# Two-network inference kernel on one core: steps of the recurrent layer's end, the final branch and the expert gather in another order and form

## The chip, the cores and the metric

The kernel runs on one core of one Trainium2 chip. The time is the device time of one execution in microseconds (us), of which the median of several runs is given. TensorE (PE) multiplies, VectorE (DVE) and ScalarE (ACT) work on what it leaves in its eight PSUM banks, GpSimd (POOL) works on SBUF alone, and SyncE (SP) issues the loads of the weights.

## The reference, cut to what matters

Two small transformer stacks stand one behind the other, on 256 tokens of width 1024. The first has two layers (a GQA mixer and an MLA mixer, each with a convolutional feed-forward part). The second has two layers: layer 0 mixes with a chunked gating unit beside a recurrent layer (RWKV-7) and ends in a SwiGLU; layer 1 mixes with sparse attention beside a short convolution and ends in a mixture of 8 experts, of which each token takes 2. The change touches the end of the recurrent layer, the experts, and the final norm.

```python
# layer 0 of the second stack
ya = _chunked_sgu(...)                    # 512 columns
yb = _rwkv7_time_mix(...)                 # 512 columns: recurrence, then a norm per head, bonus and gate
h = h + concatenate([ya, yb]) @ e_w_out[i]
...
def _moe_swiglu(h, w_router, b_router, w_gate, w_up, w_down):
    logits = xf @ w_router + b_router
    top_val, top_idx = lax.top_k(logits, TOP_K)          # TOP_K = 2 of N_EXPERTS = 8
    gates = jax.nn.softmax(top_val, axis=-1)
    ...                                                  # rows of each expert gathered
    return (jax.nn.silu(xb @ w_gate[e]) * (xb @ w_up[e])) @ w_down[e]   # EXPERT_DIM = 1408
...
return _rms_norm(h, final_norm)
```

## The kernel before

**Layout.** Activations lie transposed: `x` and `h` hold 8 tiles of 128 features by 512 columns, of which the second stack uses the 256 columns of the real tokens. Each engine has a program of its own that is written out by hand (`tensor`, `scalar`, `vector`, `gpsimd`, `sync`), and semaphores named by events (`did`, `at`) tie them together. Nothing is scheduled by a planner: what stands first in an engine's program is done first.

**Weights.** All weights come in the order of use as 1 MB chunks through a ring of 4 (`load_chunks` on SP). A chunk is two units of 128x1024. Nearly all products are made to about fp32 precision from two fp32r parts (fp32r is the type of the one-pass product; plain f32 operands take two matmul records each in the profile): `hi_units` on ACT writes the high part of a unit (`WHI`), `lo_units` on DVE subtracts it from the unit to get the low part (`WLO`), and `mm3` on PE adds three products (high by high, high by low, low by high) at L77, L78 and L79. There are 4 buffers for units, so ACT can be at most 4 units ahead, and a ring slot is free again when its second low part is made.

**End of the recurrent layer.** `solve_*` runs the recurrence for two chunks of 128 tokens (c = 0, 1). The norm of chunk 0 is done in between (the `early` generators). What is left behind the solve is `rwkv_out_*`: on PE `mean_pe(1)`, `var_pe(1)` and `roots_pe(1)`, each waiting for DVE or ACT (centre, square, root, reciprocal), then `scale_out_dve(1)`, `gate_out_dve(1)` and the two parts of the result in `HHI` and `HLO`. Only then comes `out_pe` for `e_w_out`: `project_block` makes 4 groups of output columns at once, over k = 0 to 7, with 12 matmuls for each k. Of these, k = 0 to 3 need only the gating unit's half (`yl` 0 to 3, low parts made by POOL), k = 4 to 7 need both chunks of the recurrent half (`yl` 4 and 5). The first four units of `e_w_out` are prepared by ACT and DVE behind the solve.

**Experts.** `router_*` computes logits, the two experts of each token and the places of the tokens, and `HT`, the tokens turned to rows in plain f32. `experts` then runs over e = 0 to 7 in the order `up(i)`, perhaps `scatter`, `gather(i + 1)`, `down(i - 1)`. `gather(e)` on PE multiplies `HT` with the 0/1 matrix `PP` of expert e (16 f32 matmuls of 128 columns); ACT takes the high part from PSUM (`XSHI`), DVE the low part (`XSLO`). Behind them PE turns `PP` (`PPT`, for the scatter) and makes the gate of each gathered token (`GP`). `up(e)` is three blocks of 512, 512 and 384 columns for gate and up weights each, `down(e)` two groups of 512 columns, over 33 units per expert together. The second operand of `XSP` has room for two experts, so gathering for e + 1 and using e do not collide.

**End.** The last squares and sums give the final norm's root (ACT) and reciprocal (DVE, `recip_dve(11)`). If an expert had over 128 tokens, a second pass over all experts follows (`second_pass`, an If on each engine with an Else that raises the skipped semaphores); it is not run here. PE then spreads the reciprocal (`spread_pe(12)`), DVE applies it to 8 tiles, and SP and ACT store one half each.

```python
def second_pass(lane, most, done, body):
    lane.wait_ge(*at(*done))           # PE: ss 11 7, ACT: root 11, DVE: rt 11
    with lane.e.If(most > CAP):
        body(lane, 1)
```

## Time and profile before

| what | us |
|---|---|
| median of 3 runs (2142.18 to 2147.69) | 2145.52 |
| the profiled execution | 2143.13 |
| its span | 2141.2 |
| around the span (2143.13 - 2141.2) | 1.9 |

The profile is one execution. The rows of a timeline give start, length, engine, line and operation of instructions in order of time, and in brackets how long the engine had been idle and what released it. PE rows give the matmuls; as they are pipelined, the pace is read from the distance of two starts and not from a row's length. Lines are those of helpers, so instructions are told by their tiles: `R` and `SM` are working areas, `C` and `CR` constants, `ps` a PSUM bank. A matmul of plain f32 operands shows as two records.

### The profile page before, as it was taken

Reading aid. Unit: us, or ns where it says so; the run is one execution under the profiler, and the core shown is the slowest. Engines: PE = TensorE matmul, PEld = TensorE weight load, DVE = VectorE, ACT = ScalarE, POOL = GpSimd, SP = SyncE. Lnnn points to the kernel's source line nnn. Section 1 sums busy time; section 2 is a strip of 40 time slices with the busy share of each in tenths; the row PEclk is TensorE's granted clock in tenths of the full one; section 3 lists DMA queues with packets and bytes.
Section 4 is the critical chain, followed back from the end, with each engine's and each line's share of the span. In section 5 each row is a group of like instructions: output and inputs, shape, how many; then the busy total and the mean of one; then the engine's idle time right before and its main releaser. Section 6 shows DMA issues by size and latency. Waiting matters only on the chain.

```text
span 2141.2 us, 32979 instructions
## 1 busy us (share of the span) xinstructions
PE 1999.1 (93%) x13572; PEld 1705.9 (80%) x13572; DVE 1318.8 (62%) x1992; ACT 1050.2 (49%) x1688; POOL 293.4 (14%) x303
## 2 busy tenths in 40 slices
PE   5999889999999899999998979999888899999997
PEld 2775568888778756899988869999876788888886
DVE  3238545776454458577557545444566678888886
ACT  3246533333344236566446324444445567676774
POOL 1201132111000410322013212111101000000000
PEclk9999999999999899999999889999998999999998
DMA  8332443554222121255534013545442578888783
GB/s 330 115 122 99 158 177 118 196 179 175 86 91 99 46 98 41 99 180 191 199 139 157 3 41 129 185 173 198 167 184 71 193 293 323 324 314 334 311 327 149
DMA packets 52669, 364.83 MB, mean 170 GB/s; under 512 B 5920, under 2 KB 8224, under 8 KB 8864
## 3 DMA queue, kind: packets, MB, share of 16 engines
q1 hardware_dynamic: 49488, 357.06, 45.2%
q10 hardware_dynamic: 3024, 5.58, 0.7%
q8 instruction: 110, 1.80, 0.3%
q14 instruction: 47, 0.39, 0.1%
HBM read 361.57 MB, written 1.05 MB: 169 GB/s over the span
## 4 chain that ended last, share of the span: by engine, by line
PE 83%; DVE 8%; issue 3%; ACT 3%; POOL 2%; DMA 1%; DVEq 0%; POOLq 0%; ACTq 0%; SPq 0%
PE ps L77 22%; PE ps L79 21%; PE ps L78 21%; PE ps L74 17%; DVE WLO L91 3%; PE ps L82 2%; ACT R L85 1%; DVE SM L105 1%; DVE R L91 1%; POOL R L91 1%; POOL h L95 1%; ACT WHI L85 1%; DMA ring<-W 1%; DVE x L88 0%; DVE h L88 0%
## 5 line engine op out<-in xcount | busy, mean ns | idle before, releaser
L91 DVE TENSOR_TENSOR WLO<-ring,WHI 128x1024 fp32r<-128x1024 f32 x557 | 674.7, 1247 | 203.3 <-ACT WHI L85 202.6
L85 ACT ACTIVATE WHI<-ring 128x1024 fp32r<-128x1024 f32 x557 | 567.9, 1053 | 114.7 <-PE ps L79 112.8
L77 PE MATMUL ps<-HHI,WHI 128*128 128x256 f32 (+1 forms) x1680 | 545.3, 325 | 29.8 <-DVE HLO L88 15.0
L78 PE MATMUL ps<-HLO,WHI 128*128 128x256 f32 (+1 forms) x1744 | 557.0, 319 | 0.0
L79 PE MATMUL ps<-HHI,WLO 128*128 128x256 f32 (+1 forms) x1680 | 538.3, 320 | 0.0
L77 PEld LDWEIGHTS ps<-HHI,WHI 128*128 128x128 f32 x1680 | 326.9, 195 | 69.5 <-issue 38.7
L78 PEld LDWEIGHTS ps<-HLO,WHI 128*128 128x128 f32 x1744 | 339.4, 195 | 20.0
L79 PEld LDWEIGHTS ps<-HHI,WLO 128*128 128x128 f32 x1680 | 326.3, 194 | 21.4
L74 PE MATMUL ps<-R 64*64 64x64 f32 (+9 forms) x2736 | 224.0, 286 | 5.6 <-ACT R L85 2.5
L74 PEld LDWEIGHTS ps<-R 64*64 64x64 f32 (+4 forms) x2736 | 167.6, 155 | 45.3 <-issue 36.3
L85 ACT ACTIVATE R<-ps 128x256 f32<-128x256 f32 (+5 forms) x240 | 113.0, 474 | 158.3 <-PE ps L74 94.5
L85 ACT ACTIVATE R<-ps,VEC 128x512 f32<-128x512 f32 (+1 forms) x106 | 69.1, 660 | 244.3 <-PE ps L79 243.1
L91 POOL TENSOR_TENSOR R<-R 128x256 f32<-128x256 f32 (+1 forms) x99 | 106.5, 1078 | 556.4 <-ACT R L85 555.9
L88 DVE SCALAR_TENSOR_TENSOR R<-ps,VEC,R 128x510 f32<-128x510 f32 (+1 forms) x176 | 107.9, 616 | 99.6 <-ACT R L85 95.6
L77 PE MATMUL ps<-WHI,XSHI 128*128 128x512 f32 (+3 forms) x416 | 154.9, 372 | 4.5 <-DVE WLO L91 4.2
L79 PE MATMUL ps<-WHI,XSLO 128*128 128x512 f32 (+3 forms) x416 | 150.4, 362 | 0.0
L78 PE MATMUL ps<-WLO,XSHI 128*128 128x512 f32 (+3 forms) x416 | 150.1, 361 | 0.0
L91 POOL TENSOR_TENSOR HLO<-h,HHI 128x256 fp32r<-128x256 f32 (+1 forms) x69 | 68.6, 1004 | 330.8 <-ACT HHI L85 328.4
L82 PEld LDWEIGHTS ps<-C,R 128*128 128x128 f32 x504 | 59.5, 145 | 56.2 <-issue 24.5
L77 PE MATMUL ps<-HID,WHI 128*128 128x256 f32 x352 | 100.2, 285 | 0.0
L82 PE MATMUL ps<-C,R 128*128 128x128 f32 x504 | 74.1, 286 | 27.4 <-DVE R L95 8.2
L79 PE MATMUL ps<-HID,WLO 128*128 128x256 f32 x352 | 99.6, 283 | 0.0
(171 smaller groups left out, 2819.0 us busy)
## 6 DMA issues: line engine op xcount, KB each, us to landing
ring<-W SPq DMA_DIRECT2D x340, 1024.0 KB, 4.9
x<-xt ACTq DMA_DIRECT2D x1, 2048.0 KB, 14.8
CR<-const_nsa ACTq DMA_DIRECT2D x1, 560.0 KB, 5.7
out<-x SPq DMA_DIRECT2D x1, 512.0 KB, 3.0
out<-x ACTq DMA_DIRECT2D x1, 512.0 KB, 3.0
CR<-const_rw ACTq DMA_DIRECT2D x1, 448.0 KB, 3.2
CR<-const_gqa ACTq DMA_DIRECT2D x1, 320.0 KB, 17.0
CR<-const_mla ACTq DMA_DIRECT2D x1, 320.0 KB, 2.9
```

Source lines behind the costliest of these rows:

```text
L74: return self.e.matmul(out, lhsT, rhs, start=start, stop=stop)
L77: self.e.matmul(out, l[0], r[0], start=start, stop=False)
L78: self.e.matmul(out, l[0], r[1], start=False, stop=False)
L79: return self.e.matmul(out, l[1], r[0], start=False, stop=stop)
L82: return self.e.transpose(out, in_, ident)
L85: return self.e.activation(out, in_, func, **kw)
L88: return self.e.scalar_tensor_tensor(out=out, in0=in0, scalar=s, in1=in1, op0=op0, op1=op1)
L91: return self.e.tensor_tensor(out, in0, in1, op)
L95: return self.e.tensor_scalar(out, in0, s1, None, op0)
L105: return self.e.tensor_reduce(out, in_, AX, ALU.max, negate=negate)
```

## The change

There are five edits.

1. **Weights of `e_w_out` and the gate of chunk 0, earlier.** ACT makes the first two high units before it waits for `wt_pe` of chunk 1, the other two before `nu_pe`. DVE makes the four low units and `gate_out_dve(0)` before it waits for `y_pe` of chunk 1.
2. **The recurrent layer's last steps inside the projection block.** `mean_pe(1)`, `var_pe(1)` and `roots_pe(1)` are issued ahead of the matmuls of k = 0, 1 and 2 of `project_block`. The high and low part of chunk 0 are made between the other steps.
3. **Tokens in two parts.** `HT` becomes `HTHI` and `HTLO` in fp32r (4 more subtractions of 128x512 on DVE), and `PP` becomes `PPR` in fp32r for two experts side by side. The high product goes to `XSHI` through ACT, the low product to `XSLO` through a copy on DVE.
4. **Two experts gathered at a time**: before `up(0)` and after `up(1)`, `up(3)` and `up(5)`: 32 fp32r matmuls of 256 columns each. Turning `PPR` and the gates (`spread`) come later, behind the first pair of groups of each even expert, as 2 fp32r matmuls of 128 columns and 4 of 2 columns per expert. `XSP` now has room for one pair.
5. **The end.** The branch on DVE stands ahead of the last reciprocal, on PE behind `spread_pe(11)`; there is no Else; SP stores both halves, and the result goes to columns 0 to 255 of `x`.

```diff
@@ def project_block
         for k in range(K):
+            if step:
+                step(k)
             for ev in needs(k):
@@ def solve_act
+            if c:
+                hi_units(a, L["e_out"].first[0:2])
             a.wait_ge(*at("wt_pe", c))
             a.act(WT, bank("wt", c)[:, :], ACT.Copy).then_inc(*did("rhs", ("wt", c)))
+            if c:
+                hi_units(a, L["e_out"].first[2:4])
             a.wait_ge(*at("nu_pe", c))
@@ def solve_dve
+            else:
+                lo_units(v, L["e_out"].first[0:2])
+                gate_out_dve(v, 0)
+                lo_units(v, L["e_out"].first[2:4])
             v.wait_ge(*at("y_pe", c))
@@
-    def rwkv_out_pe(pe):
-        mean_pe(pe, 1)
-        var_pe(pe, 1)
-        roots_pe(pe, 1)
+    def rwkv_out_steps(pe, k):
+        if k == 0:
+            mean_pe(pe, 1)
+        if k == 1:
+            var_pe(pe, 1)
+        if k == 2:
+            roots_pe(pe, 1)
@@ def rwkv_out_act
         spread_act(a, 1)
+        y_high_act(a, 0)
         root_out_act(a, 1)
-        for c in range(2):
+        y_high_act(a, 1)
@@ def rwkv_out_dve
-        gate_out_dve(v, 0)
         centre_dve(v, 1)
+        y_low_dve(v, 0)
         recip_out_dve(v, 1)
         scale_out_dve(v, 1)
         gate_out_dve(v, 1)
+        y_low_dve(v, 1)
@@ def router_dve
+        tokens_low(v, 0)
         v.wait_ge(*at("place"))
         step(v.cp, pos, rows3(bank("place")[:, 0:16], 8))
-        places_dve(v, 0, 0)
+        for e in range(2):
+            places_dve(v, 0, e)
+        tokens_low(v, 1)
@@ def experts
-            if i + 1 < 8:
-                gather(i + 1)
+            if i in (1, 3, 5):
+                gather((i + 1) // 2)
@@ def experts_pe
+        def gather(p):
+            for e in (2 * p, 2 * p + 1):
+                pe.wait_ge(*at("places", r, e))
+            for i, name in enumerate(("hi", "lo")):
+                for kk in range(4):
+                    b = take(pe, ("gx" + name, r, p, kk), ("x" + name, r, p, kk))
+                    for k in (2 * kk, 2 * kk + 1):
+                        for c in range(2):
+                            pe.wait_ge(*at("ht" + name, c, k // 4))
+                            t = pe.mm(b[:, 256 * (k % 2):256 * (k % 2) + 256], HTP[i][:, c, 128 * k:128 * k + 128],
+                                      PPR[:, c, :], c == 0, c == 1)
+        def spread(p):
+            pe.wait_ge(*at("weights"))
+            for e in (2 * p, 2 * p + 1):
+                b = take(pe, ("pgt", r, e), ("pgt", r, e))
+                for c in range(2):
+                    pe.mm(b[:, 128 * c:128 * c + 128], PPR[:, c, of_pair(e)], IDM, True, True)
+                for c in range(2):
+                    for i in range(2):
+                        t = pe.mm(b[:, 256:258], PPR[:, c, of_pair(e)], GGP[i][:, c, 2 * p:2 * p + 2], c + i == 0, c + i == 2)
@@ def up (PE, and on ACT behind the silu)
+                    elif nb == 0 and e % 2 == 0:
+                        spread(e // 2)
@@ def up (DVE)
-                if nb == 1 and e < 7:
-                    places(e + 1)
+                if nb < 2 and e in (1, 3, 5):
+                    places_dve(v, r, e + 1 + nb)
@@ def vector
-        recip_dve(v, 11)
-        second_pass(v, most, ("rt", 11), second_dve)
-        apply_dve(v, 12)
+        second_pass(v, most, second_dve)
+        last_recip_dve(v)
+        apply_dve(v, 11)
@@ def tensor
-        second_pass(pe, most, ("ss", 11, 7), second_pe)
-        spread_pe(pe, 12)
+        spread_pe(pe, 11)
+        second_pass(pe, most, second_pe)
```

**DVE at the end of the recurrent layer.** The difference of the two programs there. `R<-R,VEC x4` with `h<-R` is `gate_out_dve`, `COPY R<-ps` is the copy of chunk 1's result, `R<-ps,R` the centring, `HLO<-h,HHI` the low part of a chunk.

```order
-L99 COPY R<-ps 128x4x128
-L91 TENSOR_TENSOR WLO<-ring,WHI 128x1024 x4
+L91 TENSOR_TENSOR WLO<-ring,WHI 128x1024 x2
 L88 SCALAR_TENSOR_TENSOR R<-R,VEC 128x128 x4
 L91 TENSOR_TENSOR h<-R 128x4x128
+L91 TENSOR_TENSOR WLO<-ring,WHI 128x1024 x2
+L99 COPY R<-ps 128x4x128
 L88 SCALAR_TENSOR_TENSOR R<-ps,R 128x4x128
+L91 TENSOR_TENSOR HLO<-h,HHI 128x4x128
 L102 RECIPROCAL SM<-SM 128x8
```

The four low units and the gate of chunk 0 have moved ahead of the copy, so the centring follows the copy at once; one low part has moved in ahead of the reciprocal.

**PE at the first gather, before.** From the matmuls that give the places to the first product of expert 0.

```order
L74 MATMUL ps<-R,CR 128x8
L74 MATMUL ps<-R,C 128x8 x2
L74 MATMUL ps<-R 128x128 x16
L82 MATMUL ps<-C,R 128x128 x2
L74 MATMUL ps<-R 128x1 x2
L77 MATMUL ps<-WHI,XSHI 128x512
```

**PE at the same place, in the changed kernel.**

```order
L74 MATMUL ps<-R,CR 128x8
L74 MATMUL ps<-R,C 128x8 x2
L74 MATMUL ps<-PPR,HTHI 128x256 x16
L74 MATMUL ps<-PPR,HTLO 128x256 x16
L77 MATMUL ps<-WHI,XSHI 128x512
```

The 16 f32 matmuls for one expert have become 32 fp32r matmuls for two, and the turning and the gates have left this place.

**DVE at the end, before.** The rows behind the last additions to `x`; between the two L3380 rows stands the body of the second pass, which is left out here by starting anew.

```order
L102 RECIPROCAL SM<-SM 128x2
L3380 UNCONDITIONAL_BRANCH
L3385 UNCONDITIONAL_BRANCH
L88 SCALAR_TENSOR_TENSOR x<-x,VEC,ps 128x256 x8
L3671 UNCONDITIONAL_BRANCH
```

**DVE at the end, in the changed kernel.** The first reciprocal is the last instruction of the second pass, the second one that of `last_recip_dve`.

```order
L102 RECIPROCAL SM<-SM 128x2
L3440 UNCONDITIONAL_BRANCH
L102 RECIPROCAL SM<-SM 128x2
L88 SCALAR_TENSOR_TENSOR x<-x,VEC,ps 128x256 x8
L3733 UNCONDITIONAL_BRANCH
```

The reciprocal that is run when no second pass is needed now stands behind the branch, directly ahead of the 8 tiles.

## Rows read from the trace of the kernel before

**Rows 1.** The page: busy time, share of the span and instructions of each engine.

```profile
PE 1999.1 (93%) x13572; PEld 1705.9 (80%) x13572; DVE 1318.8 (62%) x1992; ACT 1050.2 (49%) x1688; POOL 293.4 (14%) x303
```

**Rows 2.** Timeline of PE, end of the recurrent layer and the block of `e_w_out`.

```profile
1268.63 1.16 PE L74 MATMUL ps<-R,C 128*128 128x128 f32 x8 [0.78 <-DVE R L99]
1278.44 1.87 PE L74 MATMUL ps<-C,R 128*128 128x2 f32 x8 [8.64 <-ACT R L85]
1280.90 1.97 PE L74 MATMUL ps<-C,SM 128*64 128x128 f32 x16 [0.60 <-DVE SM L102]
1282.80 0.58 PE L77 MATMUL ps<-HHI,WHI 128*128 128x256 f32 x1
...
1286.17 0.34 PE L77 MATMUL ps<-HHI,WHI 128*128 128x256 f32 x1
...
1307.46 0.50 PE L74 MATMUL ps<-C,R 128*128 128x1 f32 x4
```

**Rows 3.** Timeline of DVE in the same stretch.

```profile
1267.89 0.69 DVE L99 COPY R<-ps 128x512 f32<-128x512 f32 x1 [10.96 <-PE ps L74]
1268.61 6.74 DVE L91 TENSOR_TENSOR WLO<-ring,WHI 128x1024 fp32r<-128x1024 f32 x4
...
1284.08 1.14 DVE L88 SCALAR_TENSOR_TENSOR R<-R,VEC 128x128 f32<-128x128 f32 x4
...
1285.86 1.47 DVE L91 TENSOR_TENSOR HLO<-h,HHI 128x512 fp32r<-128x512 f32 x2
```

**Rows 4.** Timeline of ACT in the same stretch.

```profile
1260.44 0.60 ACT L85 ACTIVATE R<-ps 128x512 f32<-128x512 f32 x1 [3.00 <-PE ps L74]
```

**Rows 5.** Stretches of 3 us: busy PE, PEld, DVE, ACT, POOL; PE clock, DMA share, GB/s.

```profile
1257.00:1260.00 3.00, 3.00 (x29) 3.00 (x29) 0.00 (x0) 0.43 (x2) 0.00 (x0) 1.00 0.00 0
...
1278.00:1281.00 3.00, 1.97 (x10) 1.88 (x12) 0.20 (x1) 1.04 (x3) 0.00 (x0) 0.50 0.51 216
```

**Rows 6.** Timeline of PE and DVE, the first gather.

```profile
1680.86 5.47 PE L74 MATMUL ps<-R 128*128 128x128 f32 x32 [0.91 <-DVE R L96]
...
1686.74 0.48 PE L77 MATMUL ps<-WHI,XSHI 128*128 128x512 f32 x1
...
1680.20 0.60 DVE L96 TENSOR_SCALAR R<-CR,R 128x128 f32<-128x128 f32 x2
```

**Rows 7.** Timeline of PE, the gather for expert 1.

```profile
1719.44 3.73 PE L74 MATMUL ps<-R 128*128 128x128 f32 x32
1723.01 0.38 PE L82 MATMUL ps<-C,R 128*128 128x128 f32 x2
1723.23 0.50 PE L74 MATMUL ps<-R 128*128 128x1 f32 x4
1723.60 0.47 PE L77 MATMUL ps<-WHI,XSHI 128*128 128x512 f32 x1
...
1725.76 0.39 PE L77 MATMUL ps<-WHI,XSHI 128*128 128x512 f32 x1
```

**Rows 8.** Experts: stretches (as rows 5), then waits (1740 to 2100), two groups (1800 to 2000).

```profile
1900.00:2000.00 100.00, 98.84 (x531) 84.97 (x530) 83.39 (x87) 68.31 (x82) 0.00 (x0) 1.00 0.82 314
...
1820.00:1824.00 4.00, 4.00 (x20) 3.30 (x19) 3.65 (x4) 2.73 (x5) 0.00 (x0) 1.00 1.01 422
...
PE ps L77 <- DVE WLO L91: 3.9, 12, 0.4
...
L91 DVE TENSOR_TENSOR WLO<-ring,WHI 128x1024 fp32r<-128x1024 f32 x120 | 139.0, 1220 | 6.5 <-ACT WHI L85 6.4
L85 ACT ACTIVATE WHI<-ring 128x1024 fp32r<-128x1024 f32 x119 | 119.4, 1055 | 8.3 <-PE ps L79 7.5 <-DMA ring<-W 0.5
```

**Rows 9.** Timeline of DVE and PE at the end, and the branch's row on PE.

```profile
2129.32 0.17 DVE L102 RECIPROCAL SM<-SM 128x2 f32<-128x2 f32 x1 [4.23 <-ACT SM L85]
...
2133.30 1.22 PE L74 MATMUL ps<-C,SM 128*128 128x128 f32 x4 [4.32 <-DVEq L3387]
...
L3380 PEldq COMPARE_BRANCH  x1: 3637/3637/3637, 2129.0 to 2129.0; - x1
```

More of the change, by code:

```diff
@@ L569, in program @@
     YSP = [over("YS" + n, "R2", 3584 + 2048 * i, 2048, F32R)[:, :].rearrange("p (a n) -> p a n", n=1024)
+           for i, n in enumerate(("HI", "LO"))]
+    IDM = over("IDM", "R2", 7688, 128, F32R)[:, :]
+    GGP = [over("GG" + n, "R2", 7816 + 16 * i, 16, F32R)[:, :].rearrange("p (c n) -> p c n", c=2)
            for i, n in enumerate(("HI", "LO"))]
@@ L1094, in summed_after, with out_pe @@
         return min(j, 2 * (j - st.side + 1)) if st.side else j
-    def out_pe(pe, key, st, N, X, needs, c, before=None):
+    def out_pe(pe, key, st, N, X, needs, c, before=None, step=None):
         done = 0
         if st.side:
-            project_block(pe, st, [(("group", key, j), ("x", key, j), N, X) for j in range(st.side)], needs)
+            project_block(pe, st, [(("group", key, j), ("x", key, j), N, X) for j in range(st.side)], needs, step)
         for j in range(st.side, 8):
@@ L3062, in router_pe @@
             for half in range(2):
-                b = take(pe, ("ht", c, half), ("ht", c, half))
+                b = take(pe, ("ht", c, half), ("htlo", c, half))
                 for k in range(4):
@@ L3115, in router_dve, with tokens_low, gates_dve, step @@
         v.tt(rm[:, 2:4], rm[:, 2:4], rm[:, 0:2], ALU.subtract).then_inc(*did("route", ("gap",)))
+        tokens_low(v, 0)
         v.wait_ge(*at("place"))
         step(v.cp, pos, rows3(bank("place")[:, 0:16], 8))
-        places_dve(v, 0, 0)
+        for e in range(2):
+            places_dve(v, 0, e)
+        tokens_low(v, 1)
+        step(v.rmax, rm[:, 8:9], bank("place")[:, 16:24])
+        v.cp(FLAG[:, :], rm[:, 8:9]).then_inc(*did("flag", ("flag",), ("flag0",)))
+    def tokens_low(v, c):
+        for half in range(2):
+            z = slice(512 * half, 512 * half + 512)
+            v.wait_ge(*at("hthi", c, half))
+            v.tt(HTP[1][:, c, z], bank("ht", c, half)[:, :], HTP[0][:, c, z], ALU.subtract).then_inc(
+                *did("tokens_lo", ("htlo", c, half)))
+    def gates_dve(v):
+        def step(op, *a, **kw):
+            op(*a, **kw).then_inc(*did("route"))
+            v.wait_ge(*last("route"))
         v.wait_ge(*at("gap_exp"))
@@ L3295, in up @@
                     *did("silu", ("silu_m", r, e, nb)))
+                if nb == 0 and e % 2 == 0:
+                    spread(e // 2)
         def down(e):
@@ L3314, in experts_dve, with gather @@
             lo_units(v, st.first)
-        def places(e):
-            if (r, e) != (0, 0):
-                places_dve(v, r, e)
-        def gather(e):
-            i = e % 2
-            if e == 0:
-                places(0)
-            for half in range(2):
-                v.wait_ge(*at("xhi", r, e, half))
-                v.tt(XSP[1][:, i, 4 * half:4 * half + 4, :], rows3(bank("gx", r, e, half)[:, :], 128),
-                     XSP[0][:, i, 4 * half:4 * half + 4, :], ALU.subtract).then_inc(*did("x_lo", ("xlo", r, e, half)))
+        def gather(p):
+            if p:
+                v.wait_ge(*at("mup", r, 2 * p - 1, 2, 1))
+            elif r:
+                for e in range(2):
+                    places_dve(v, r, e)
+            for kk in range(4):
+                v.wait_ge(*at("gxlo", r, p, kk))
+                v.cp(XSP[1][:, 2 * kk:2 * kk + 2, :], rows3(bank("gxlo", r, p, kk)[:, :], 256)).then_inc(
+                    *did("x_lo", ("xlo", r, p, kk)))
+            if (r, p) == (0, 0):
+                gates_dve(v)
         def turn(e, nb):
@@ L3373, in fullest, with second_pass @@
         return lane.e.value_load(FLAG[0:1, 0:1], min_val=0, max_val=256)
-    def second_pass(lane, most, done, body):
-        lane.wait_ge(*at(*done))
-        start, seen = dict(S.n), dict(lane.past)
+    def second_pass(lane, most, body):
+        seen = dict(lane.past)
         with lane.e.If(most > CAP):
@@ L3382, in second_pass @@
         lane.past = seen
-        raised = [(name, n - start.get(name, 0)) for name, n in S.n.items() if n > start.get(name, 0)]
-        if raised:
-            with lane.e.Else():
-                for name, n in raised:
-                    lane.e.sem_inc(S.sem(name), n)
     def last_sums_pe(pe, r):
@@ L3399, in second_pe @@
     def second_pe(pe, r):
+        keep(bank_of["rs", 11])
         experts_pe(pe, r)
         last_sums_pe(pe, r)
+        pe.wait_ge(*at("rt", 11 + r))
+        for i in range(2):
+            t = pe.mm(ps[bank_of["rs", 11]][:, 128 * i:128 * i + 128], RT[:, i:i + 1].broadcast_to([128, 128]), ident,
+                      True, True)
+        t.then_inc(*did("spread", ("rs", 11 + r)))
     def second_act(a, r):
```

128 lines of the change are left out of this document (60 added, 68 removed).

## The prediction

> **What bounds the kernel now.** I read the page first: TensorE is busy for 93% of the span and no other engine for more than 62% [rows 1], so a step counts by what it adds to PE's own row or by how long PE stands idle for it. Then I read PE's timeline at the three places that the change touches, with DVE's and ACT's beside it, to see what ends each idle time. At the end of the recurrent layer PE does a mean of 1.16 us, stands idle for 8.64 us, and then works at half clock, since the granted clock in 1278 to 1281 is 0.50, the lower of the two levels [rows 2, 5]. In the experts PE is 98.8% busy at full clock, and waits for low weight parts 12 times by 3.9 us in 360 us [rows 8]: what shortens PE's work there shortens the span, as long as the weights keep up. At the very end PE waits 4.32 us between a reciprocal and four records that spread it [rows 9].
>
> **The recurrent layer's end (edits 1 and 2).** Before, DVE copies chunk 1's result (done at 1268.6) and then makes four low units (6.74 us) and the gate of chunk 0 before it centres chunk 1 [rows 3]; that is PE's idle time. All of it moves ahead of the copy. There DVE had been idle for 10.96 us [rows 3], and four units at 1.22 us (the group's mean without POOL beside it [rows 8]) and a gate of 1.8 us (1284.08 to 1285.86 [rows 3]) take 6.7 us. ACT has 3.0 us free from 1257.4 on [rows 4] for two high units of 1.05 us [rows 8], and about as much again behind `wt_pe` for the other two. The DMA share in 1257 to 1260 is 0.00 [rows 5], so the chunks have landed. I cost the moved work at nothing; if ACT came late, the solve would wait by up to one high unit, 1 us.
>
> Now PE's new order. One k of the block is 12 matmuls, and from 1286.17 to 1307.46 PE does 177 of them without a gap (81 of the block, 96 of the four groups behind it), 0.120 us each, so 1.44 us for a k [rows 2]. The mean is done at 1269.8. While PE does k = 0 (to 1271.2), DVE centres (0.7, as the copy) and ACT squares (0.6, as its 128x512 copy [rows 4]), to 1271.1. The variance at full clock is half of 1.87 [rows 2], to 1272.2; root and reciprocal lie beside k = 1 (to 1273.7); the roots are half of 1.97, to 1274.7. DVE scales (1.1) and gates (1.8) to 1277.6, while PE does k = 2 and 3, to 1277.6 as well. High and low part and two hand-overs take 1.6, PE waits that long, and k = 4 to 7 end at 1279.2 + 5.8 = 1285.0. Before, the block ends at 1307.46 - 96 x 0.120 = 1295.9. The gain is 10.9; I take **10.5**, as each hand-over costs a little. If PE stays at half clock until k = 3, 48 matmuls cost 0.10 us more each (15 took 3.37 us from 1282.80 on [rows 2]), and variance and roots 1.9 more, of which the wait of 1.6 hides a part: the gain is then about 5.5. What is late next is DVE's scaling and gating of chunk 1, which nothing shortens.
>
> **The gather (edits 3 and 4).** An expert's gather takes PE from 1719.44 to 1723.60, 4.16 us, of which 3.57 are the 32 records of 16 f32 matmuls [rows 7]. In their place stand 32 fp32r matmuls of 256 columns for two experts. That form costs 0.120 us in the block [rows 2]: 3.84 us for a pair. Turning and gates become 4 matmuls of 128 and 8 of 2 columns per pair. The trace has neither of exactly this form here; the upper bound is 0.12 each for the first, and for the second the 0.09 of the four records with one column (1723.23 to 1723.60 [rows 7]), together 1.2 us; the lower bound is half of it, 0.6. I take 1.1, the row that is nearest. So a pair costs 3.84 + 1.1 = 4.9 us instead of 8.3, a gain of 3.4, and three such pairs give 10.1.
>
> The first pair stands on a chain of waits. Before, PE starts at 1680.86 and is at the first product at 1686.74, 5.88 us later [rows 6]; the same work takes 4.16 later on, as its 32 records take 5.47 us here and 3.73 there [rows 6, 7]. Afterwards two more place matrices stand ahead of it (0.30 us each [rows 6]); two of the four new subtractions (0.7 each) lie beside PE's matmuls for the places, the other two beside the high products. PE then needs 3.84 x 5.47/3.73 = 5.6 us, plus 1.1 for the part that comes later: 7.3 instead of 5.88 + 4.16 = 10.0, a gain of 2.7. Together **12.8**.
>
> What could take it back is the supply of weights. A unit costs PE six matmuls, about 1.4 us (nine from 1723.60 to 1725.76 [rows 7]), DVE 1.22 and ACT 1.05 [rows 8]. In `spread`, ACT stands behind its silu until PE has finished the second product of an even expert, and only then copies and goes on with high units. At that time two of the coming group's units are ready, 2.8 us of PE's work; ACT needs about 0.6 for the copies that are left and 1.05 for the unit, DVE 1.22 more: 2.9 to 3.2 us. That is a wait of 0.1 to 0.4 us, four times. In return the place matrices no longer stand in DVE's row in the even experts' second blocks, where some of the 12 short waits lie [rows 8]. I set these two against each other at 0; the bounds are a gain of 1 and a loss of 6 us (one unit of 1.4 us at each spread). Queued behind ACT's new wait are the high units, behind them DVE's low units, and behind those SP's ring slots.
>
> **The end (edit 5).** PE's branch takes 3.6 us, and the spread starts at 2133.30, though the reciprocal was done at 2129.49 [rows 9]. Afterwards PE spreads first and branches later, when nobody waits for it. DVE branches before the reciprocal, where it is idle for 4.23 us [rows 9], so from 2125.1 to 2128.7 at PE's length, before the root. The spread can start some 0.15 us behind the reciprocal, at 2129.64: a gain of **3.7**. SP storing both halves moves the second issue from ACT to an idle queue; between 0 and 0.5 us, taken as 0. On the branch the Trainium skill (Advanced Engine Details and Errata, Control Flow Timing) gives about 108 ns for a compare-and-branch. By that, the branch would not explain PE's wait, the edit would bring about 0.7 us, and the sum would be 3 us smaller. The row shows 3637 ns and decides; the skill's page Runtime: NRT & Kernel Launch, Instruction fetch mechanics, has a reason that fits it, that a taken branch to a page not yet fetched waits for the fetch.
>
> **Sum.** 10.5 + 12.8 + 3.7 = 27.0 us. The profiled execution took 2143.13 (span 2141.2 and 1.9 around it), which gives 2116.1. It lies 2.4 below the median of 2145.52, and on the median the forecast is **2118.5**.
>
> **Rivals.**
> - *The weights fall behind in the experts.* For it: DVE is busy for 83.4 of 100 us [rows 8] and waits for ACT, which has a new wait. Against it: the waits so far are 0.3 us each. One unit lost at each spread and half of one at each gather gives about 8 us: 2126.5. Chance 0.12.
> - *The clock stays low at the recurrent end.* PE's records before the mean are small ones, and the clock was half after the idle time [rows 5]. But the idle time goes, and the 5 us are lost only if the lower level covers the whole of k = 0 to 3: 2123.5. Chance 0.09.
> - *The branch on DVE is still on the way*, because it starts later than I read. It would do no more than hold the reciprocal back by its length: 2122. Chance 0.05.
> - *The ring is too small for the longer stretches.* With a gather only every second expert, PE asks for 66 units (34.6 MB) in some 93 us, 370 GB/s, where the mean was 314. The transfers reach 422 in a stretch of 4 us [rows 8], so they should follow. If 314 were the limit, three chunks ahead would leave 31.5 MB, 100 us instead of 93, three times: 2139.5, no change. Chance 0.04.
> - *Slower than before.* ACT's wait at the spread uses up the lead of the units for good: from there PE waits for each high and low part in turn, 1.05 + 1.22 + hand-overs, 2.4 us a unit instead of 1.4. At 1.0 us lost per unit it decides from 27 + 6.4 us on, a little over 8 units after each of the four spreads; with 12 units each it costs 48 us: 2166.5. Against it: DVE is faster than PE by 0.2 us per unit and so regains a lead. Chance 0.04.
>
> **How the numbers follow.** The forecast as worked out has 0.66. About 0.3% (6.4 us) is what a measurement of this kernel can tell from no change. Faster by more: 0.66 + 0.12 + 0.09 + 0.05 = 0.92; same 0.04; slower 0.04. Low end: half price for turning and gates (2 us), the first gather at the later ones' pace (2), the short waits gone (1) and the lowest of the runs instead of their median (3.3) reach 2110. High end: the first two rivals together lose 13 us, so 2131. That leaves the last two cases and about 0.1 beyond both ends out.
>
> **What would show it.** Right: PE's idle time of 8.64 us behind the mean is gone, with one wait of 1 to 2 us ahead of k = 4, and the block ends 10 to 11 us earlier as against the mean; a pair's gather is 3.8 us of PE and the spread about 1.1; PE's spread starts 0.2 us behind the last reciprocal. Wrong: waits of PE for `WLO` in the experts of well over 4 us, most of them behind the spreads; a granted clock of 0.50 beside k = 0 to 3; ACT waiting for the ring; a clock below 1.00 in the experts, which nothing here allows for.

## The result and the profile after

The changed kernel takes 2116.64 us (median of 4 runs, 2115.12 to 2120.84); the kernel before, beside it, 2143.85 (4 runs, 2141.59 to 2147.69). The ratio is 0.9876, 95% interval 0.9863 to 0.9889. The forecast was 2118.5 in a range of 2110 to 2131. The profiled execution took 2117.42, with a span of 2115.5 against 2141.2: 25.7 us less, where the prediction's sum was 27.0.

To see where these 25.7 us are, I use DVE's reciprocals as marks. Both programs run 67 of them in the same order, so the k-th of one answers to the k-th of the other. The stretches between seven marks follow (starts from DVE's timeline, all in us); the NSA layer is layer 1 of the second stack, the one with sparse attention:

```
                                 before    after   before   after   gain
                                 start     start   stretch  stretch
last one ahead of the solve      1248.94   1248.64  1248.94  1248.64   0.30
behind the block of e_w_out      1310.90   1299.76    61.96    51.12  10.84
attention of the NSA layer       1602.32   1591.36   291.42   291.60  -0.18
the same, four reciprocals on    1622.28   1613.44    19.96    22.08  -2.12
ahead of the router              1666.79   1657.18    44.51    43.74   0.77
the last one                     2129.32   2105.81   462.53   448.63  13.90
end of the span                  2141.2    2115.5     11.9      9.7    2.2
```

So the recurrent end gave 10.8, the experts 13.9, the end 2.2, and a stretch that no edit touches, inside the attention of the NSA layer, lost 2.1.

**Recurrent end.** PE's timeline of the changed kernel (start, length, engine, line, operation, shapes, count, idle time before it and what ended it), answering to [rows 2]:

```profile
1268.33 1.16 PE L74 MATMUL ps<-R,C 128*128 128x128 f32 x8 [0.78 <-DVE R L99]
...
1270.93 1.05 PE L74 MATMUL ps<-C,R 128*128 128x2 f32 x8
...
1273.45 1.09 PE L74 MATMUL ps<-C,SM 128*64 128x128 f32 x16
...
1279.11 0.35 PE L77 MATMUL ps<-HHI,WHI 128*128 128x256 f32 x1 [1.50 <-DVE HLO L91]
```

The wait of 8.64 us is gone, the variance takes 1.05 us where it took 1.87 and the roots 1.09 for 1.97, so the clock is full; the one wait left is 1.50 us ahead of k = 4. On DVE ([rows 3] before) the units and the gate now lie in the idle time ahead of the copy:

```profile
1258.24 2.36 DVE L91 TENSOR_TENSOR WLO<-ring,WHI 128x1024 fp32r<-128x1024 f32 x2 [1.61 <-ACT WHI L85]
...
1267.58 0.69 DVE L99 COPY R<-ps 128x512 f32<-128x512 f32 x1 [2.93 <-PE ps L74]
```

**Experts.** PE's timeline at the first gather (answering to [rows 6]), at the turning and gates of a later pair, and at a later gather (answering to [rows 7]). The later gather is 32 matmuls, of which 16 take 1.92 us (1850.56 to 1852.48), so 3.84 us for a pair:

```profile
1668.82 0.36 PE L74 MATMUL ps<-R,CR 128*128 128x8 f32 x2 [1.48 <-DVE R L91]
...
1676.94 0.40 PE L77 MATMUL ps<-WHI,XSHI 128*128 128x512 f32 x1
...
1775.02 0.34 PE L74 MATMUL ps<-IDM,PPR 128*128 128x128 f32 x2
...
1775.38 0.25 PE L74 MATMUL ps<-GGHI,PPR 128*128 128x2 f32 x1
1775.49 0.25 PE L74 MATMUL ps<-GGLO,PPR 128*128 128x2 f32 x1
...
1776.28 0.48 PE L77 MATMUL ps<-WHI,XSHI 128*128 128x512 f32 x1
...
1850.56 2.08 PE L74 MATMUL ps<-PPR,HTHI 128*128 128x256 f32 x16
1852.48 2.08 PE L74 MATMUL ps<-PPR,HTLO 128*128 128x256 f32 x16
```

The waits of the same kernel from 1714 to 2074 (us in total, times, longest), beside [rows 8]: PE waits less for low parts than before (3.9 us, 12 times), ACT waits for the ring, and its new wait for the turned matrix is there, 4.5 us.

```profile
ACT WHI L85 <- DMA ring<-W: 6.8, 10, 1.4
...
ACT PPT L85 <- PE ps L74: 4.5, 6, 1.6
PE ps L77 <- DVE WLO L91: 2.8, 9, 0.4
```

**End.** The timeline of DVE and PE, and the branches of both (count: shortest, median, longest ns, first and last start), beside [rows 9]:

```profile
2105.81 0.17 DVE L102 RECIPROCAL SM<-SM 128x2 f32<-128x2 f32 x1 [4.55 <-ACT SM L85]
2106.03 1.22 PE L74 MATMUL ps<-C,SM 128*128 128x128 f32 x4 [0.55 <-DVE SM L102]
...
L3440 DVEq COMPARE_BRANCH  x1: 72/72/72, 2101.2 to 2101.2; - x1
...
L3440 PEldq COMPARE_BRANCH  x1: 3659/3659/3659, 2106.0 to 2106.0; - x1
```

PE spreads 0.2 us behind the reciprocal's start, 3.98 before: a gain of 3.76.

PE's branch was not the last thing that the spread waited for before. The chain that ended last (start, length, what) goes through DVE, whose own branch, a row of 0.07 us at 2129.52, stands ahead of these:

```profile
2129.59 3.08 issue
2132.67 0.02 DVEq L3387
...
2133.23 0.03 DVEq L3387
```

DVE's next instruction came 3.08 us behind its branch. It is the first of the eight semaphore raises of the Else (L3387), and the last of them ends at 2133.26, just ahead of the spread at 2133.30. PE's branch of 3637 ns ended at 2132.64 and its own three raises at about 2133.0. So both engines stood still for three to four microseconds at the same time, and DVE came last. The edit takes both out of the way: DVE's branch now starts at 2101.2, 4.6 us ahead of the reciprocal, in time in which DVE waits for the root anyway.

Only 2.2 of the 3.76 us reaches the end of the span, because the output lands later. The page's rows on the issues of the output (count, KB each, median us from issue to landing), before (ACT's half has the same numbers):

```profile
out<-x SPq DMA_DIRECT2D x1, 512.0 KB, 3.0
```

and in the changed kernel:

```profile
out<-x SPq DMA_DIRECT2D x2, 512.0 KB, 4.7
```

### The profile page after: what moved, and what is told of

Same layout as the page of the kernel before. It is cut to its first block, busy times and chain, and to the rows that moved or that the text cites. A ratio compares the mean times of both kernels' runs of the same rounds, so it can differ in the third digit from the quotient of the medians.

```text
span 2115.5 us, 32719 instructions
## 1 busy us (share of the span) xinstructions
PE 1986.0 (94%) x13444; PEld 1692.8 (80%) x13444; DVE 1318.4 (62%) x1997; ACT 1049.8 (50%) x1690; POOL 289.9 (14%) x303
## 3 DMA queue, kind: packets, MB, share of 16 engines
HBM read 361.57 MB, written 1.05 MB: 171 GB/s over the span
## 4 chain that ended last, share of the span: by engine, by line
PE 84%; DVE 8%; ACT 3%; issue 3%; POOL 2%; DMA 1%; DVEq 0%; POOLq 0%; ACTq 0%; SPq 0%
PE ps L77 22%; PE ps L78 21%; PE ps L79 21%; PE ps L74 17%; DVE WLO L91 3%; PE ps L82 2%; ACT R L85 1%; DVE SM L105 1%; POOL R L91 1%; ACT WHI L85 1%; DVE R L91 1%; DMA ring<-W 1%; POOL h L95 0%; DVE x L88 0%; DVE h L88 0%
## 5 line engine op out<-in xcount | busy, mean ns | idle before, releaser
L74 PE MATMUL ps<-R 64*64 64x64 f32 (+10 forms) x2448 | 189.5, 288 | 3.9 <-ACT R L85 1.7
L85 ACT ACTIVATE R<-ps 128x512 f32<-128x512 f32 (+5 forms) x236 | 110.8, 472 | 152.8 <-PE ps L74 90.3
L74 PEld LDWEIGHTS ps<-R 64*64 64x64 f32 (+5 forms) x2448 | 133.4, 151 | 44.2 <-issue 37.0
L77 PE MATMUL ps<-HID,WHI 128*128 128x256 f32 x352 | 100.2, 285 | 0.0
L78 PE MATMUL ps<-HID,WHI 128*128 128x256 f32 x352 | 99.6, 283 | 0.0
## 6 DMA issues: line engine op xcount, KB each, us to landing
x<-xt ACTq DMA_DIRECT2D x1, 2048.0 KB, 14.8
```

Source lines behind the costliest of these rows:

```text
L74: return self.e.matmul(out, lhsT, rhs, start=start, stop=stop)
L77: self.e.matmul(out, l[0], r[0], start=start, stop=False)
L78: self.e.matmul(out, l[0], r[1], start=False, stop=False)
L85: return self.e.activation(out, in_, func, **kw)
```

## The experiments

Four questions were open: does each part bring its term; which of edits 1 and 2 gives the 10.8 us, and is it the clock; what in the gather gives the gain; and why the output lands 1.7 us later. A "stretch" below is one of the table above. Ratios are against the kernel before on the same chip, with the 95% interval.

### The three parts alone

**Edits 1 and 2 alone** (the hunks of `project_block`, `solve_act`, `solve_dve` and `rwkv_out_*`; the rest as before).

> The kernel before with edits 1 and 2 alone (units and gate of chunk 0 earlier, the last steps inside the projection block). Theory (the three gains add up): 10.5 to 11 us faster than before, PE's first record behind the block 10.7 us earlier. Rival (the profile of the changed kernel was lucky in the stretch, or the gain is given back later): less than 8 us.

Measured: 2134.17 us, ratio 0.9961 (0.9948 to 0.9973). The stretch of the recurrent end is 51.13 us, a gain of 10.83, the same as in the whole. The time as a whole gives 8.4 us (5.8 to 11.1), which is below the 10.5 to 11 that I expected: part of the gain is given back later, in stretches that the last experiment section tells of.

**Edits 3 and 4 alone** (router and experts).

> The kernel before with edits 3 and 4 alone (tokens in two parts, two experts at a time). Theory: 13 to 14 us faster, all of it between the places of the tokens and the last reciprocal. Rival (part of what stands there in the changed kernel comes from the clock, which the recurrent part's edits shift): 10 us or less.

Measured: 2129.85 us, ratio 0.9938 (0.9918 to 0.9959). The stretch of the experts is 447.78 us against 462.53, a gain of 14.75. The output lands after 3.0 us.

**Edit 5 alone** (branches, reciprocal and stores).

> The kernel before with edit 5 alone (the branch, and both halves stored by SP). Theory: the spread starts 3.7 us earlier and the store of the second half gives 1.6 us of it back, so 2.1 us faster. Rival (the late landing in the changed kernel was chance): 3.7 us faster. As forecast the store would have cost 0 to 0.5 us.

Measured: 2140.23 us, ratio 0.9989 (0.9978 to 1.0). The time alone could not be told from no change, but the trace can: last reciprocal at 2133.24, PE's spread (timeline of PE) right behind it, and from the reciprocal to the end of the span 9.9 us against 11.9. The output lands after 4.1 us (page).

```profile
2133.47 1.22 PE L74 MATMUL ps<-C,SM 128*128 128x128 f32 x4 [0.55 <-DVE SM L102]
...
out<-x SPq DMA_DIRECT2D x2, 512.0 KB, 4.1
```

The three local gains are 10.8, 14.8 and 2.0 us, 27.6 in all; the ratios say 8.4 + 13.3 + 2.4 = 24.1 us, and the first of them holds the 2.1 us of the clock in the NSA layer. Each part does its work alone. Edit 5 moves DVE's branch, PE's branch and the raises of the Else together; what each of the three is worth by itself no run separates.

### Which of edits 1 and 2, and is it the clock?

**Edit 1 alone**: units and gate earlier, the steps still ahead of the block.

```diff
@@ def solve_act, solve_dve: as in the change (hi_units, lo_units and gate_out_dve(0) earlier)
@@ def rwkv_out_dve
-        gate_out_dve(v, 0)
```

> The kernel before with edit 1 alone: the units' weights and the first gate computed ahead of the solve; the steps stay outside the block, behind the group means. My theory: edits 1 and 2 gained 10.8 us together by the reciprocal marks, and edit 2 (PE has work through the variance wait, and so keeps its clock) is the larger part only together with edit 1, since the steps wait for the gate. Edit 1 alone should take the units' and gate's time off the stretch behind the solve, but leave the 8.64 us wait of the variance with PE idle and the 1.87 and 1.97 us matmul groups at 1.2 GHz: I expect 3 to 6 us by the marks. Rival (the order does not matter, only the amount of DVE work behind the solve does): the whole 10 to 11 us already here.

Measured: 2138.96 us, ratio 0.9977 (0.9967 to 0.9988). The recurrent end's stretch is 52.84 us: a gain of **9.1**, not 3 to 6. PE's timeline:

```profile
1270.98 1.05 PE L74 MATMUL ps<-C,R 128*128 128x2 f32 x8 [1.44 <-ACT R L85]
1272.63 1.98 PE L74 MATMUL ps<-C,SM 128*64 128x128 f32 x16 [0.59 <-DVE SM L102]
```

**Edit 2 alone**: the steps in the block, units and gate still behind the solve.

```diff
@@ def project_block
+            if step:
+                step(k)
@@ def rwkv_out_act, rwkv_out_dve: y_high_act(a, 0) and y_low_dve(v, 0) between the other steps
@@ def tensor
-        rwkv_out_pe(pe)
-        out_pe(pe, "e_out", ...)
+        out_pe(pe, "e_out", ..., step=lambda k: rwkv_out_steps(pe, k))
```

> The kernel before with edit 2 alone: the recurrent steps are put inside the normalisation's block, between the mean and the variance, but the units' weights and the first gate stay behind the solve. My theory: DVE's order then puts the steps' work where PE would otherwise wait for the variance, but the chain of units, gate and steps is as long as before: 3 to 7 us by the marks, and the variance's and roots' matmul groups at about 1.05 and 1.09 us where they were 1.87 and 1.97. Rival as above, the other way: 10 to 11 us already here, with edit 1 worth nothing.

Measured: 2144.39 us, ratio 1.0 (0.999 to 1.001). The stretch is 61.25 us: a gain of **0.7**. PE's timeline: k = 0 lies beside DVE's units, but the variance comes as late as before.

```profile
1266.29 1.16 PE L74 MATMUL ps<-R,C 128*128 128x128 f32 x8 [0.79 <-DVE R L99]
...
1276.09 1.86 PE L74 MATMUL ps<-C,R 128*128 128x2 f32 x8 [6.28 <-ACT R L85]
```

The mean is at 1266.29, the variance 9.8 us later, as before (1278.44 - 1268.63). So my expectation for both was wrong in the same way. The distance from mean to variance was set by DVE's row: 8.5 us of units and gate (6.74 and 1.8 [rows 3]) between the copy and the centring. Edit 1 takes that away, and the distance falls from 9.8 us to 2.6 (1268.38 to 1270.98); with the variance's group at 1.05 us instead of 1.87 and 1.1 us behind the roots this is the gain of 9.1. Edit 2 needs edit 1, and adds 1.7 to it: with both, PE's matmuls fill the waits of 1.44 and 0.59 us, and the roots run at full clock.

**PE filled through the long wait**: the kernel before with 60 matmuls that nobody reads.

```diff
@@ def rwkv_out_pe
         mean_pe(pe, 1)
+        b = take(pe, ("fill",), ("oc", 1))
+        ...
+        for i in range(60):
+            o = UNIT * (L["e_out"].first[i % 4] % UNITS)
+            pe.mm(b[:, 0:256], WHI[:, o:o + 128], WHI[:, o + 256:o + 512], True, True)
         var_pe(pe, 1)
```

> The kernel before with 60 more matmuls of 256 columns on PE between the mean and the variance of the recurrent end, whose results nobody reads (about 7.2 us at 0.120 us each, within the 8.64 us wait). No step of the kernel is moved. Theory (part of the gain at the recurrent end is TensorE's clock): the granted clock there rises from about half to full, the variance group goes from 1.87 to about 1.05 us, the roots' from 1.97 to about 1.09, the first 15 matmuls behind them to 0.12 each; about 3 us by the marks. Rival (the clock did not matter, or the fill delays the variance): 0 or a loss of up to 1 us.

Measured: 2144.56 us, ratio 1.0003 (0.9992 to 1.0013); the stretch is 61.40 us, a gain of 0.6. PE's timeline, and two stretches (busy us of PE, PEld, DVE, ACT, POOL; PE clock, DMA share, GB/s):

```profile
1268.97 7.43 PE L74 MATMUL ps<-WHI 128*128 128x256 f32 x60
1277.91 1.05 PE L74 MATMUL ps<-C,R 128*128 128x2 f32 x8 [1.51 <-ACT R L85]
1279.56 1.97 PE L74 MATMUL ps<-C,SM 128*64 128x128 f32 x16 [0.59 <-DVE SM L102]
...
1269.00:1277.00 8.00, 7.40 (x62) 7.20 (x61) 7.97 (x10) 0.00 (x0) 4.74 (x3) 1.00 0.48 160
1279.00:1284.00 5.00, 4.44 (x28) 4.11 (x29) 2.55 (x10) 0.79 (x2) 0.00 (x0) 0.50 0.01 2
```

The clock was 1.00 throughout the fill, and the variance took 1.05 us. But behind two short waits, of 1.51 and 0.59 us, it was 0.50, and PE paid there what it would have paid before. Here the busy row ahead did not keep the clock at full; in the changed kernel the block's matmuls lie in those short waits too, and the roots take 1.09 us. Of the theory that keeping PE busy through the long wait brings 3 us, 0.6 is left.

### What in the gather gives the gain?

**The pair's matmuls in two halves**: 64 of 128 columns where 32 of 256 are.

```diff
@@ def experts_pe, gather(p)
-                        for c in range(2):
-                            ...
-                            t = pe.mm(b[:, 256 * (k % 2):256 * (k % 2) + 256], ..., PPR[:, c, :], c == 0, c == 1)
+                        for e in range(2):
+                            for c in range(2):
+                                ...
+                                t = pe.mm(b[:, 256 * (k % 2) + 128 * e:...], ..., PPR[:, c, of_pair(e)], c == 0, c == 1)
```

> The changed kernel, with each of the gather's matmuls of 256 columns made as two of 128 columns, one for each expert: 64 matmuls for a pair where 32 are. Nothing else changes. Theory (the gather's gain is the width: a short fp32r matmul costs nearly what one of 256 columns does, 0.11 against 0.120 us by the two turning matmuls in the changed kernel's trace): a pair takes 64 x 0.11 = 7.0 us instead of 3.84, four pairs lose 12 to 13 us, and the experts' gain of 13.9 us is all but gone. Rival (the gain is the fp32r form with the tokens in two parts, and the cost goes by columns): 64 x 0.06 = 3.84 us for a pair, no loss.

Measured: 2137.39 us, ratio 0.9973 (0.9962 to 0.9984). The experts' stretch is 467.65 us, 19.0 more than in the changed kernel and 5.1 more than before the change. PE's timeline at the first gather, then at a later one, and a stretch beside the first:

```profile
1670.04 6.89 PE L74 MATMUL ps<-PPR,HTHI 128*128 128x128 f32 x32 [1.46 <-DVE PPR L96]
...
1683.56 0.73 PE L77 MATMUL ps<-WHI,XSHI 128*128 128x512 f32 x1
...
1862.32 3.69 PE L74 MATMUL ps<-PPR,HTHI 128*128 128x128 f32 x32
...
1869.42 0.44 PE L77 MATMUL ps<-WHI,HDHI 128*128 128x512 f32 x1
...
1671.00:1683.00 12.00, 12.00 (x58) 12.00 (x57) 2.43 (x6) 2.59 (x5) 0.00 (x0) 0.50 0.13 52
```

At a later gather the 64 matmuls take 7.10 us (1862.32 to 1869.42), 0.111 each: 3.3 more than 3.84, and three such pairs make 9.8. The first gather takes 13.52 us (1670.04 to 1683.56) instead of 5.40 (1671.54 to 1676.94, in the changed kernel), 8.1 more: PE was busy all the time, and the granted clock stayed at 0.50. The first nine products behind it are slow too, 3.85 us instead of 2.07. These three come to 19.7 us, of which 19.0 show in the stretch. The 12 to 13 us that I expected were too few, but the rival is out, and the theory's price for a short matmul was right; what it missed is the clock beside the first gather. The pairing, not the fp32r form, carries edits 3 and 4.

**Turning and gates directly behind the gather** for pairs 1 to 3.

```diff
@@ def experts
-            if i in (1, 3, 5):
-                gather((i + 1) // 2)
+            if i in (1, 3, 5):
+                gather((i + 1) // 2)
+                spread((i + 1) // 2)
```

> The changed kernel, with the turning and the gates of pairs 1 to 3 directly behind their gather instead of behind the first pair of groups; pair 0 stays. It prices where they stand, and the wait that ACT has there for PE. Theory (ACT's wait at the spread costs next to nothing, because the lead of the weights covers it): the experts take the same time within 1 us, and PE's waits for the low weight parts stay at about 9, of 0.3 us each. Rival (the place is what keeps the weights ahead, or ACT's wait is what still costs): 2 to 5 us either way, and the number or the length of PE's waits for the low parts changes with it.

Measured: 2120.73 us, ratio 0.9901 (0.9884 to 0.9917). The experts' stretch is 449.03 us against 448.63. The waits (1705 to 2090):

```profile
ACT PPT L85 <- PE ps L74: 6.1, 6, 1.8
...
PE ps L77 <- DVE WLO L91: 3.3, 10, 0.5
```

ACT waits 1.6 us more, PE 0.5 us more, and the stretch is 0.4 longer. The experts of the changed kernel and of the three variants of its end, where they are the same, took 448.11 to 448.63 us, so 0.4 is hardly more than their spread. The theory holds: ACT's wait costs next to nothing in either place.

### Why does the output land later?

**The second half stored by ACT**, as before the change.

```diff
@@ def scalar
         second_pass(a, most, second_act)
+        a.wait_ge(*at("nx", 11, 7, 0))
+        load(a, out_dram[:, 4:8, :], x[:, 4:8, 0:256], "d_out_b")
+        a.wait_ge(*at("d_out_b"))
```

> The changed kernel with the second half of the result stored by ACT again. Theory (two transfers in one queue of SP stand behind each other): the second transfer lands 3.0 us after its issue instead of 4.7, and the kernel is 1.6 us faster than the changed one, 2115.0. Rival (a transfer that ends the program takes 4.7 us by chance or since it comes second): no difference to the changed kernel.

Measured: 2118.23 us, ratio 0.9887 (0.9865 to 0.9909). From the last reciprocal (2103.52) to the end of the span (2113.2) it is 9.7 us, as in the changed kernel. The page:

```profile
out<-x SPq DMA_DIRECT2D x1, 512.0 KB, 3.5
out<-x ACTq DMA_DIRECT2D x1, 512.0 KB, 4.6
```

The queue is not the cause: one store in each is late as well.

**No branch**: the second pass and its branch are left out on all engines.

```diff
@@ def tensor, def scalar, def sync
-        second_pass(...)
@@ def vector
-        second_pass(v, most, second_dve)
-        last_recip_dve(v)
+        recip_dve(v, 11)
```

> The changed kernel without the second pass and without the branch to it on every engine (the second pass, which is not run for these inputs, is left out; the loads of its values stay). Theory (in the changed kernel the 1.7 us longer landing of the output, 4.7 where it was 3.0, is the fetch of PE's instructions behind the branch, one 16 KB packet that one DMA engine carries at the same time as a part of the output): landing of the output back to about 3.0 us and the end 1.6 us earlier against the last reciprocal. Rival (the landing is longer because of how the output is stored): 4.6 to 4.7 as before.

Measured: 2114.39 us, ratio 0.9866 (0.9849 to 0.9882). From the last reciprocal (2105.31) to the end (2113.5) it is 8.2 us, 1.5 less, and the landing is back to 3.0, with both halves still stored by SP and from the same columns of `x`, so neither of these is the cause. The DMA view of the last 13 us of this kernel (GB/s in 40 slices; its one queue, q1, has 1056 packets):

```profile
GB/s 0 0 0 0 0 0 0 0 0 0 0 0 0 0 0 0 0 0 0 0 0 0 0 0 0 22 331 353 350 347 262 350 353 353 350 158 0 0 0 0
```

and of the changed kernel, with the queues (packets, MB, share of 16 engines):

```profile
GB/s 0 0 0 0 25 0 0 0 0 0 25 0 50 0 0 0 0 0 25 0 0 217 347 340 347 287 312 378 321 328 287 22 25 22 25 19 0 0 0 0
...
q1 hardware_dynamic: 1056, 1.05, 24.5%
q8 instruction: 2, 0.03, 1.0%
```

The same 1056 packets go out at the same 350 GB/s, but in the changed kernel they end in a tail of five slices, 1.6 us, at 19 to 25 GB/s. In the tail only packets of the output move, and shortly ahead of it one instruction packet of queue 8 shares the engines with them (the same view from 2111 to 2112.5, then from 2113.2 to 2115.5):

```profile
q1 hardware_dynamic: 480, 0.48, 97.4%
q8 instruction: 1, 0.02, 4.0%
...
q1 hardware_dynamic: 34, 0.03, 4.3%
```

22 GB/s is a sixteenth of 350, so I read the 34 packets of the tail as what one of 16 engines has left when the others are done. Before, the instruction packets of the end were through ahead of the output: the view from 2130 to 2137 has both of queue 8, and the output starts at 2137.

```profile
q8 instruction: 2, 0.03, 2.1%
```

The DMA view in steps of 0.2 us shows whose packets these are. In the changed kernel the two of queue 8 are at 2107.0 and 2111.8, 1.0 and 5.8 us behind the start of PE's branch (2106.0); before, they are at 2130.0 and 2133.4, 1.0 and 4.4 us behind it (2129.0). So the first comes while PE stands in the branch, and the second behind the end of the branch (2109.7), in the middle of the output. In all six kernels with the new end and a branch (the changed one, edit 5 alone and four variants), the second packet lies in the output, and the last store has a landing of 4.1 to 4.7 us on the page. That the instruction packets behind the branches cause the late landing is shown by the branches' removal; that it is this one packet is read from its time, since the others lie ahead of the output. That a packet which takes one engine 0.96 us (4.0% of 16 engines in 1.5 us) costs 1.6 is not explained by it. The Trainium skill (Runtime: NRT & Kernel Launch, Instruction fetch mechanics) says that a taken branch to a page not in reach forces a DMA fetch; this trace agrees, with an instruction packet 1.0 us behind PE's branch, and shows whose transfers such packets can meet.

**The last piece halved**: tiles 4 and 5, then 6 and 7, as stores of 256 KB.

```diff
@@ def sync
-        s.wait_ge(*at("nx", 11, 7, 0))
-        load(s, out_dram[:, 4:8, :], x[:, 4:8, 0:256], "d_out_b")
+        s.wait_ge(*at("nx", 11, 5, 0))
+        load(s, out_dram[:, 4:6, :], x[:, 4:6, 0:256], "d_out_b")
+        s.wait_ge(*at("nx", 11, 7, 0))
+        load(s, out_dram[:, 6:8, :], x[:, 6:8, 0:256], "d_out_c")
```

> The changed kernel with the second half of the output stored in two pieces of two tiles each (256 KB), the first of them as soon as its tiles are done. Theory (what is late at the end is one DMA engine, which carries PE's 16 KB of instructions beside the output): the last piece is half as long, which saves 0.5 to 0.8 us of transfer, but the collision stays if the last piece meets the fetch, so the end comes 0.3 to 0.8 us earlier as against the last reciprocal (9.7 us from there to the end of the span in the changed kernel, 8.2 without the branch). Rival (three stores in one queue cost more than they save): 0 or up to 0.5 us later.

Measured: 2119.26 us, ratio 0.9879 (0.9852 to 0.9907). From the last reciprocal (2110.09) to the end (2119.8) it is 9.7 us: nothing gained. The DMA view of its last 13 us has the same tail, five slices at 9 to 25 GB/s. Smaller pieces did not help here; by the reading above, because the engine that is late stays late. No version beat the changed kernel with its function whole.

### The stretch that no edit touches

The two microseconds lost in the NSA layer do not look like chance. Each kernel has one profile, and that stretch took 19.96 to 20.01 us in the three profiles whose recurrent end is as before (the kernel before, edits 3 and 4 alone, edit 5 alone), and 22.06 to 23.01 in all ten whose recurrent end differs, even in the one with only the 60 unread matmuls. PE's timeline before, and after:

```profile
1611.00 1.09 PE L82 MATMUL ps<-C,R 128*128 128x128 f32 x8 [0.98 <-DVE R L91]
```

```profile
1610.16 1.92 PE L82 MATMUL ps<-C,R 128*128 128x128 f32 x8 [0.97 <-DVE R L91]
```

The windows of both from 1611 on, before and then after, show the granted clock (the last number but two):

```profile
1611.00:1614.00 3.00, 3.00 (x28) 2.22 (x30) 2.25 (x11) 0.89 (x4) 0.00 (x0) 1.00 0.00 0
```

```profile
1611.00:1614.00 3.00, 3.00 (x23) 2.20 (x21) 1.71 (x10) 3.00 (x4) 0.00 (x0) 0.56 0.03 5
```

The work and the waits (0.98 and 0.97 us) are alike, only the clock differs. The end of the experts' stretch shows a smaller loss of the same kind. Its last 38 us, in the kernel with edits 3 and 4 alone and then in the changed kernel, have the same matmuls and the same idle time of PE, but 0.9 us more of busy time and a lower granted clock (the last number but two):

```profile
2076.38:2114.16 37.78, 36.00 (x185) 30.56 (x183) 28.84 (x31) 23.93 (x32) 0.00 (x0) 0.97 0.44 167
```

```profile
2067.18:2105.81 38.63, 36.87 (x185) 31.36 (x183) 28.79 (x31) 23.91 (x32) 0.00 (x0) 0.95 0.44 165
```

That is why the experts gain 14.8 us alone and 13.9 in the changed kernel; with edits 1 and 2 alone the experts' stretch grows by 0.9 us too (463.39 against 462.53).

That it is the clock is shown; why it falls there is open, and the code ahead is not the whole answer. The variant without a branch has the changed kernel's program up to the end, yet its recurrent stretch took 52.78 us instead of 51.12: counted from the last reciprocal ahead of the solve, its granted clock was 0.50 from 14 to 20 us, where the changed kernel's was 0.52 from 14 to 17 us and 1.00 from 17 to 20. Its stretch in the NSA layer took 22.97 us instead of 22.08.

## Why the prediction was right, step by step

- **Recurrent end, 10.5 (10.9 worked out).** Measured 10.84. The variance, roots, the wait ahead of k = 4 (1.6 forecast, 1.50) and the moved work at no cost all came as said. My expectations of the experiments were wrong in one thing that the sum does not need: the two edits are not two halves; edit 1 alone brings 9.1.
- **The clock stays low there** (a rival): did not come. The roots took 1.09 us.
- **A pair's gather, 3.84.** Measured 3.84.
- **Turning and gates, 1.1 per pair.** Measured 1.27 (1775.02 to the next product), above my upper bound of 1.2. The term failed at the gate's matmuls: those with 2 columns follow each other at 0.11 us, where I had taken 0.09. A pair gained 3.2, not 3.4; three make 9.6, not 10.1.
- **First pair, 2.7.** From the first matmul for the places to the first product it takes 8.12 us (1668.82 to 1676.94); before, 8.04 from 1678.70. With 4.16 for the second expert then and 1.27 for turning and gates now, 12.20 against 9.39: a gain of 2.8.
- **Weights set at net 0, bounds a gain of 1 and a loss of 6.** Measured a gain of 1.1: PE's waits for `WLO` are 2.8 us instead of 3.9. This is the favourable end of the bounds. 9.6, 2.8 and 1.1, and 0.3 ahead of the places, make 13.8, and the clock of the last 38 us takes 0.9 back, so of the 13.9 measured some 1 us is not accounted for. I had forecast 12.8: part of the agreement is luck, as a gain that I do not know of and a loss of clock that I did not foresee nearly cancel. ACT's new wait (the rivals of 2126.5 and 2166.5) cost nothing that could be found, and ACT waits 6.8 us for the ring without PE's waits growing: the ring is late at times, but not on the way (the rival of 2139.5).
- **Branch and spread, 3.7.** Measured 3.76, and the size was right, but the wait had a second cause that the sum does not name. It put the wait down to PE's branch; DVE stood still behind its own branch for 3.08 us and raised the last semaphore at 2133.26, some 0.2 us later than PE was ready. The forecast still holds because edit 5 moves both branches, and because I had costed DVE's at PE's length when I moved it into idle time. The Trainium skill (Advanced Engine Details and Errata, Control Flow Timing) gives about 108 ns for a compare-and-branch. DVE's row of 72 ns is near it and PE's of 3659 ns is not; but a branch's row is not its cost here, since the 3.08 us behind DVE's are in no row. By that figure the edit would have brought about 0.7 us; 3.76 were measured.
- **SP storing both halves, 0 to 0.5, taken as 0.** This failed: the landing cost 1.6 us. I looked at the queue that issues, and it is not the queue: moving PE's branch behind the spread moved its second instruction packet into the store. I had written that PE branches later, "when nobody waits for it"; the output did.
- **Not in the sum**: 2.1 us of clock in the NSA layer, 0.3 us gained ahead of the solve, and 0.6 in the stretches around the NSA layer (0.77 - 0.18). With 0.3 more at the recurrent end, 1.1 more in the experts and 1.5 less at the end this makes 25.7 of 27.0 in the profiled execution; by the ratio it is 26.6 us (23.8 to 29.4).

## What to carry to other kernels

When a wait is long, list what stands between its two ends on the engine that ends it: moving that work earlier gained 9.1 us, filling the wait with other matmuls 0.6. Merge small matmuls until they are wide, since a matmul of 128 columns cost 0.11 us here and one of 256 columns 0.12. Where a branch is moved out of the way, ask when its instruction packets come, up to 5.8 us behind the branch here, and which transfers share the DMA engines at that time. And look for the cost of a branch in the gap behind its row too.

## What the runs showed of the hardware

- With a 16 KB instruction packet in the middle of the output's store, the landing took 4.1 to 4.7 us instead of 3.0, and in the changed kernel 34 packets were left for a tail at 19 to 25 GB/s. Without the branches the landing was 3.0 again.
- The branch over the second pass took 3637 and 3659 ns on PE in the kernels before and after. On DVE its row is 72 ns, but before the change the next instruction followed only 3.08 us behind it.
- The granted clock fell to 0.50 behind waits of 1.51 and 0.59 us, though PE had been busy for 7.40 of 8 us until 2 us before. At the first gather it stayed at 0.50 through 12 us in which PE was wholly busy with matmuls of 128 columns; in the changed kernel, with matmuls of 256 columns, it was at 1.00 again 5 us after they had begun.
- One stretch of unchanged code, 300 us behind a changed place, ran at another clock in ten of ten kernels, at a cost of 2.1 to 3.0 us. But the clock also differed between the changed kernel and the one without a branch in code that is the same in both, by 1.7 us in the recurrent layer.
